# Running the second half of an expert slot one pair later in a layer with gathered experts

## What is computed

```python
mixed = gates[0] * (o_sb @ w_o_sb) + gates[1] * (o_sw @ w_o_sw) + gates[2] * (o_mem @ w_o_mem)
x = x + mixed @ w_out                       # the merge
q = (rmsnorm(x) @ w_q).reshape(t, 8, 2, 128)
s = einsum('thpd,hpkd->thpk', q, keys)      # 8 heads, 2 x 128 key scores
v1, i1 = top_k(s[:, :, 0], 16); v2, i2 = top_k(s[:, :, 1], 16)
best, flat = top_k(v1[..., :, None] + v2[..., None, :], 16)
idx = e1 * 128 + e2                         # 128 experts for each token
g = softmax(best)
a = gelu(einsum('thkd,td->thk', u_tab[idx], xb))
y = x + einsum('thk,thkd->td', g * a, v_tab[idx])
```

## Time and profile before

| | |
|---|---|
| median of 3 runs | 4426.72 us (4423.26 to 4434.2) |
| the profiled execution | 4421.1 us, its span 4419.2 us |
| busy: PE, DVE, ACT, POOL | 3611.0, 2811.9, 1235.3, 1836.7 us |
| granted TensorE clock, mean | 0.923 |
| moved by DMA | 1415.44 MB, of which 1208.03 MB by the gathers |
| 1152 gathers | first issued at 1145.6 us, last at 4389.4 us |
| DVE: 1152 dots of 1217 ns | idle before them 556.1 us, of which 548.7 us for a gather |
| PE: 3520 matmuls of L1375 | idle before them 688.4 us, of which 667.1 us for a diagonal |

### The profile page before, as it was taken

How to read it: one execution, slowest core, us unless ns; L and a number is a source line. 1 busy time by engine, 2 the same in 40 slices (tenths; PEclk the granted TensorE clock), 3 DMA queues, 4 the chain that set the end, 5 groups by cost and what they waited for, 6 DMA issues and landing times.

```text
span 4419.2 us, 34952 instructions
## 1 busy us (share of the span) xinstructions
PE 3611.0 (82%) x11113; PEld 1885.0 (43%) x11113; DVE 2811.9 (64%) x6038; ACT 1235.3 (28%) x2663; POOL 1836.7 (42%) x1477
## 2 busy tenths in 40 slices
PE   7999798989768797867898878996787777787777
PEld 4545457778534345432333335442233233233222
DVE  2130541821698965886996997687677676676554
ACT  2111772620332233332223224333111112112111
POOL 0000340000366576656666666666433333333332
PEclk9999996989889999988999999998899999999999
DMA  3202102234799899989999999999999999999998
GB/s 123 69 25 80 30 1 86 84 122 162 293 351 391 319 405 421 396 333 421 421 419 421 412 420 415 422 411 409 421 421 421 417 412 418 415 413 414 421 421 354
DMA packets 249160, 1415.44 MB, mean 320 GB/s; under 512 B 26624, under 2 KB 59648, under 8 KB 95872
## 3 DMA queue, kind: packets, MB, share of 16 engines
q0 software_dynamic: 165888, 1208.03, 66.6%
q1 hardware_dynamic: 83088, 205.18, 12.6%
HBM read 1374.85 MB, written 39.19 MB: 320 GB/s over the span
## 4 chain that ended last, share of the span: by engine, by line
DMA 23%; POOL 18%; DVE 13%; PE 12%; issue 11%; ACT 2%; POOLq 0%; SPq 0%; ACTq 0%; DVEq 0%
DMA ring<-in_experts_dram,idx 22%; POOL side L1265 10%; POOL ring L1254 8%; PE ps L1375 7%; DVE ring L1618 5%; PE ps L1298 2%; PE ps L1323 1%; DVE wgt L1624 1%; PE ps L1346 1%; PE ps L1308 1%; ACT diag L1468 1%; DVE hot L1507 1%; DVE hot L1510 1%; DVE e L1512 1%; DVE flat L1503 0%
## 5 line engine op out<-in xcount | busy, mean ns | idle before, releaser
L1375 PE MATMUL ps<-ring,diag 128*128 128x512 f32 x3520 | 1792.9, 654 | 688.4 <-ACT diag L1468 667.1
L1254 POOL DMA_INDIRECT ring<-in_experts_dram,idx x1152 | 1096.1, 952 | 1905.9 <-PE ps L1375 1334.5
L1618 DVE CUSTOM_DVE_ANT_0 ring<-ring,ps 128x1024 f32<-128x1024 f32 x1152 | 1381.7, 1217 | 556.1 <-DMA ring<-in_experts_dram,idx 548.7
L1375 PEld LDWEIGHTS ps<-ring,diag 128*128 128x128 f32 x3520 | 695.3, 206 | 1693.2 <-ACT diag L1468 948.7
L1265 POOL TENSOR_TENSOR side<-side,ring 128x1024 f32<-128x1024 f32 x272 | 640.8, 2356 | 42.6 <-ACT ring L1473 37.4
L1457 ACT ACTIVATE act_<-hid 128x2 f32<-128x2 f32 x576 | 117.1, 203 | 1773.5 <-DVE hid L1618 1772.8
L1468 ACT ACTIVATE diag<-const,wgt 128x128 f32<-128x128 f32 x880 | 319.4, 395 | 482.8 <-DVE wgt L1624 480.2
L1298 PE MATMUL ps<-hx,wbuf 128*128 128x256 f32 (+2 forms) x1152 | 403.1, 495 | 13.3 <-DMA hx<-hT_scratch 13.1
L1624 DVE TENSOR_TENSOR wgt<-act_,gw 128x2 f32<-128x2 f32 x576 | 240.9, 418 | 124.9 <-ACT act_ L1457 121.6
L1473 ACT ACTIVATE ring<-ring,wgt 128x1024 f32<-128x1024 f32 x272 | 308.4, 1134 | 0.0
L1298 PEld LDWEIGHTS ps<-hx,wbuf 128*128 128x128 f32 x1152 | 225.6, 196 | 184.5 <-issue 119.3
(11 more groups left out here) (187 smaller groups left out, 3096.6 us busy)
## 6 DMA issues: line engine op xcount, KB each, us to landing
wbuf<-in_w_gate_o_dram SPq DMA_DIRECT2D x72, 768.0 KB, 8.3
wbuf<-in_w_q_dram SPq DMA_DIRECT2D x24, 1024.0 KB, 9.0
ring<-in_experts_dram,idx POOLq DMA_INDIRECT x1152, 16.0
wbuf<-in_w_out_dram SPq DMA_DIRECT2D x12, 1024.0 KB, 8.9
w_qkv<-in_w_in_dram SPq DMA_DIRECT2D x5, 2048.0 KB, 8.0
o_x<-o_scratch SPq DMA_DIRECT2D x9, 768.0 KB, 25.2
s<-s_scratch SPq DMA_DIRECT2D x6, 1024.0 KB, 11.6
hT_scratch<-hT SPq DMA_DIRECT2D x9, 512.0 KB, 7.0
```

The lines of the kernel that those rows point to most:

```text
L1254: i = nc.gpsimd.indirect_dma_start(out=ring[:, j % RING, :], out_offset=None, in_=A["experts"], in_offset=bass.IndirectOffsetOnAxis(ap=idx ...
L1375: last = nc.tensor.matmul(acc[:, h, :], diag[:, (by_pe(j) - 1) % 4, :], ring[:, j % RING, DM + h * HB:DM + (h + 1) * HB], start=(j % SLOTS ...
L1618: last = nc.vector.tensor_tensor_reduce(out=u, in0=u, in1=xp, scale=1.0, scalar=0.0, op0=ALU.mult, op1=ALU.add, accum_out=hid[:, j % SLOTS ...
```

## The change

The pair of a slot's second half is now the pair before the one whose dots are being made. With Q = 64 m + q counting the pairs of all tiles:

- DVE: dots of Q, product of Q - 1, piece of the search, `finish` of the tile before (now at q = 1), advance. The last product stands alone behind the loop. The copy to `xp` waits for its own engine's `dots` as well.
- ACT: gelu of Q, then diagonals and scaled rows of Q - 1, then advance.
- PE: advance for Q, then the matmuls of Q - 1.

POOL and SP are as they were, and no instruction is added or taken away.

```diff
--- before.py
+++ after.py
@@ -1377,13 +1377,11 @@
                     last.then_inc(pe_done, 1)
 
             advance(0)
-            for m in range(NT):
-                for q in range(NB):
-                    if q == 0:
-                        advance(1 + m * NB)
-                    accumulate(m, q)
-                    if q:
-                        advance(1 + m * NB + q)
+            for Q in range(NT * NB + 1):
+                if Q < NT * NB:
+                    advance(1 + Q)
+                if Q:
+                    accumulate((Q - 1) // NB, (Q - 1) % NB)
 
         @block.scalar
         def _(act):
@@ -1450,27 +1448,33 @@
 
             advance = walk(front)
             advance(0)
-            for m in range(NT):
-                for q in range(NB):
+            def spread(m, q):
+                act.wait_ge(weights, m * NB + q + 1)
+                for j in range(m * SLOTS + q * BATCH, m * SLOTS + (q + 1) * BATCH):
+                    if sided(j):
+                        continue
+                    d = by_pe(j) - 1
+                    if d >= 4:
+                        act.wait_ge(pe_done, d - 3)
+                    last = nc.scalar.activation(diag[:, d % 4, :], ident, ACT.Copy, scale=wgt[:, j % SLOTS:j % SLOTS + 1])
+                last.then_inc(diags, 1)
+                for j in range(m * SLOTS + q * BATCH, m * SLOTS + (q + 1) * BATCH):
+                    if sided(j):
+                        v = ring[:, j % RING, DM:2 * DM]
+                        nc.scalar.activation(v, v, ACT.Copy, scale=wgt[:, j % SLOTS:j % SLOTS + 1]).then_inc(scaled, 1)
+
+            for Q in range(NT * NB + 1):
+                m, q = Q // NB, Q % NB
+                if Q < NT * NB:
                     c = slice(q * BATCH, (q + 1) * BATCH)
-                    act.wait_ge(dots, m * NB + q + 1)
+                    act.wait_ge(dots, Q + 1)
                     nc.scalar.activation(act_[:, c], hid[:, c], ACT.Gelu_apprx_tanh).then_inc(gelus, 1)
-                    advance(1 + m * NB + q)
+                if Q:
+                    spread((Q - 1) // NB, (Q - 1) % NB)
+                if Q < NT * NB:
+                    advance(1 + Q)
                     if q == TOP_FROM[m] + 24 * TOP_EVERY[m] + 1 and m + 1 < NT and m + 1 not in FIRST_OF:
                         exponentiate(m + 1, None)
-                    act.wait_ge(weights, m * NB + q + 1)
-                    for j in range(m * SLOTS + q * BATCH, m * SLOTS + (q + 1) * BATCH):
-                        if sided(j):
-                            continue
-                        d = by_pe(j) - 1
-                        if d >= 4:
-                            act.wait_ge(pe_done, d - 3)
-                        last = nc.scalar.activation(diag[:, d % 4, :], ident, ACT.Copy, scale=wgt[:, j % SLOTS:j % SLOTS + 1])
-                    last.then_inc(diags, 1)
-                    for j in range(m * SLOTS + q * BATCH, m * SLOTS + (q + 1) * BATCH):
-                        if sided(j):
-                            v = ring[:, j % RING, DM:2 * DM]
-                            nc.scalar.activation(v, v, ACT.Copy, scale=wgt[:, j % SLOTS:j % SLOTS + 1]).then_inc(scaled, 1)
 
         @block.vector
         def _(dve):
@@ -1594,6 +1598,12 @@
                         weigh(f.base, f.weigh[tau])
                     yield
 
+            def product(Q):
+                m, q = Q // NB, Q % NB
+                dve.wait_ge(gelus, Q + 1)
+                c = slice(q * BATCH, (q + 1) * BATCH)
+                nc.vector.tensor_tensor(wgt[:, c], act_[:, c], gw[:, m % 2, c], ALU.mult).then_inc(weights, 1)
+
             def finish(m):
                 last = m * SLOTS + SLOTS - 1
                 dve.wait_ge(pe_done, by_pe(last))
@@ -1607,6 +1617,8 @@
             spilled = 0
             for m in range(NT):
                 dve.wait_ge(x_in, 16 * (m + 1))
+                if m:
+                    dve.wait_ge(dots, m * NB)
                 nc.vector.tensor_copy(xp, xrow[:, :]).then_inc(x_taken, 1)
                 dve.wait_ge(x_taken, m + 1)
                 follow = m + 1 < NT and m + 1 not in FIRST_OF
@@ -1618,10 +1630,8 @@
                         last = nc.vector.tensor_tensor_reduce(out=u, in0=u, in1=xp, scale=1.0, scalar=0.0, op0=ALU.mult, op1=ALU.add,
                                                               accum_out=hid[:, j % SLOTS:j % SLOTS + 1])
                     last.then_inc(dots, 1)
-                    advance(1 + m * NB + q)
-                    dve.wait_ge(gelus, m * NB + q + 1)
-                    c = slice(q * BATCH, (q + 1) * BATCH)
-                    nc.vector.tensor_tensor(wgt[:, c], act_[:, c], gw[:, m % 2, c], ALU.mult).then_inc(weights, 1)
+                    if m or q:
+                        product(m * NB + q - 1)
                     c = q - TOP_FROM[m]
                     k = TOP_EVERY[m]
                     if follow and 0 <= c < 24 * k and c % k == 0:
@@ -1632,8 +1642,10 @@
                         shift(m + 1, None)
                     if follow and c == 24 * k + 2:
                         weigh(m + 1, None)
-                    if q == 0 and m:
+                    if q == 1 and m:
                         finish(m - 1)
+                    advance(1 + m * NB + q)
+            product(NT * NB - 1)
             finish(ST)
```

## The result

The change makes the kernel slower: 4472.85 us in the median of 4 runs (4469.81 to 4476.75) against 4425.0 of the kernel before beside it (4423.26 to 4434.2), a ratio of 1.0104 [1.0087, 1.0122]. The profiled execution took 4476.75 us, its span 4474.9, at a mean clock of 0.918. Forecast were 4435 us and a range from 4403 to 4468.

A forecast was written before the change was run, and what follows sets the result against it. Gathers were taken to bound the kernel behind 2030 us, VectorE three earlier stretches. Terms 0 + 0 + 5 + 15 + 3.7 - 4.5 - 5 - 6 = +8 us, against the 4426.7 median, gave 4435 us, range 4403 to 4468.

The forecast's parts named there:

- Tiles 2 to 4: ... I take 5 us: In tiles 2 to 4, gathers left with too little backlog lose 5 us, bounds 0 and 53 us.
- A slot's release moves by the same 4.7 us: Everywhere, a pair's product starts 4.7 us later, so its slot's release and next gather also come 4.7 us later.
- the 2.2 us for each piece: Tiles 2 to 4: most lost at each of 24 long search pieces, from the least gather latency; at most 53 us.
- Tiles 5 to 7, tile 8: 0: Tiles 5 to 8: gather latencies fall by 4.7 us but stay over 5.4, so the later release costs nothing.
- The tail: +3.7: Kernel end: the matmuls of the pair before run first, the last pair's follow, plus 3.7 us.
- Gelu waits: -4.5: Second and third stretches bound by VectorE: the product's wait for the gelu goes, 4.5 us saved.
- DVE's waits for ACT's merge steps: -5: Second and third stretches bound by VectorE: 12.2 us of waits shrink, 5 us saved, bounds -12 and some +5.
- The product held up by POOL's additions: -6: Stretches bound by VectorE: additions meet dots oftener and hold the product up less, 6 us saved, bounds -30 and +10.
- The three stretches: +15: 1196 to 1280, 1400 to 1560, 1840 to 1960 us, bound by VectorE: two fewer landed slots cost 5 us each time.
- The ring starves: Tiles 2 to 4 and the three stretches: ring of 10 too short, 4457 us at half the bound; chance 0.38.
- VectorE's relief wins: Three stretches bound by VectorE: fewer waits and hold-ups there win 28 us, 4399 us; chance 0.22.
- Nothing but the tail: Whole kernel: ring stays full, only 3.7 us added at the end, 4430 us; part of the case given 0.40.

The follow-up runs named there:

- lag_only: The changed kernel with the merge's steps put back where they were before, leaving only the lag of one pair: 4484.65 us, 1.0142 to the kernel before.
- after_ring11: The changed kernel with 11 ring slots instead of 10, three small search buffers moved into unused constants: 4439.72 us, 1.0039 to the kernel before.

## Why the prediction was wrong

**The failed step** is the term "Tiles 2 to 4: ... I take 5 us". It measured +44 (24.7 + 15.4 + 3.7). Two things in it were wrong.

The first is the row it leaned to. "Being nearer to the median's row" takes the median latency of the earlier trace rows, 4.5 us in hand; but a short queue comes back behind nearly every one of the 8 long pieces of a tile, and is paid there: 24.7/8 = 3.1 us for each in tile 2, 1.9 in tile 3, not the loss of a rare gather. A dip that comes with a period has to be priced at the least, whatever the median says.

The second is the step under it, "A slot's release moves by the same 4.7 us", for every pair. It holds for the median pair (product 0.28 us behind its dots before, 4.9 after), but not for the one ahead of a long piece: its product moved by 11.5 us in tile 2 and 8.9 in tile 3. So the 2.2 us for each piece were no upper bound. Tile 2 lost more than that; the 53 us hold 8 pieces of tile 4, which lost but 3.7, and the 16 of tiles 2 and 3 have a bound of 35 and lost 40.

With 44 in place of 5 the sum would have been +47; measured were 4472.85 - 4425.0 = +48. That they agree so well is in part luck, for the tiles add up to 55.7: the terms for the three stretches (15 - 4.5 - 5 - 6) forecast nothing, and tiles 0 and 1 lost 9.2.

Two things stood in the text and were passed over. At the long piece of tile 5 it says "the same gap now falls on the pair before, with one pair fewer under way". With the lag, the pair ahead of the piece is held across it, and PE has only the pair before that one to work on. What that does to a release was bounded there for tiles 5 to 7 and not carried over to tiles 2 to 4, where less is in hand. That PE stands still for 7 us and starts again at 1.2 GHz, with 8 matmuls in 6.62 us for 3.70, was not considered at all. And the item's other ground, "part of the delay there was paid already (ACT waited with its diagonals behind merge steps...)", holds only for tile 4: its long pieces, those of the next group's first search, stood between dots and product before the change too, and it lost 3.7 us.

**By its other steps:**

- *Tiles 5 to 7, tile 8: 0.* Right: -0.4, 0.0, -0.2 (tile 8's +3.3 is the tail), and 417 GB/s. There the pieces have the same instructions, but POOL adds almost nothing, the product ahead of a piece waits 8.4 us at most, and the backlog is deeper. The 4.7 us less latency show at the end: the last gather was issued at 4389.42 before and its dots started at 4408.80, 19.4 us later; after, 4447.56 to 4461.35 is 13.8. That is 5.6 less.
- *The tail: +3.7.* Right, +3.3. The last rows of the changed kernel, which answer to the earlier trace rows:

```profile
4461.35 1.22 DVE L1630 CUSTOM_DVE_ANT_0 ring<-ring,ps 128x1024 f32<-128x1024 f32 x1 [1.25 <-DMA ring<-in_experts_dram,idx]
...
4463.46 7.13 PE L1375 MATMUL ps<-ring,diag 128*128 128x512 f32 x16 [1.26 <-ACT diag L1459]
...
4470.63 1.23 DVE L1613 TENSOR_TENSOR side<-ps,side 128x1024 f32<-128x1024 f32 x1 [7.61 <-PE ps L1375]
```

  Sixteen matmuls for eight, and `finish` waits 7.61 us, where "some 8" was forecast.
- *Gelu waits: -4.5.* They are gone: the whole kernel has 0.2 us of them.
- *DVE's waits for ACT's merge steps: -5.* 2.5 us in the second stretch for 4.1, 2.3 in the third for 8.1, so -7.4: right. The waits of VectorE in the two stretches after:

```profile
DVE gt L1565 <- ACT gt L1401: 2.5, 2, 2.0
...
DVE v L1493 <- ACT mixn L1436: 2.3, 1, 2.3
```

- *The product held up by POOL's additions: -6.* Wrong in sign. The groups of 1150 to 1600, as in the earlier trace rows:

```profile
L1630 DVE CUSTOM_DVE_ANT_0 ring<-ring,ps 128x1024 f32<-128x1024 f32 x127 | 150.8, 1217 | 41.0 <-DMA ring<-in_experts_dram,idx 39.0 <-DVE gw L1544 1.2 <-DVE gw L1537 0.2
L1605 DVE TENSOR_TENSOR wgt<-act_,gw 128x2 f32<-128x2 f32 x62 | 54.6, 880 | 0.0
L1568 DVE TENSOR_TENSOR mixn<-mixn,gt 128x384 f32<-128x384 f32 x12 | 15.4, 1285 | 0.4
```

  880 ns for 753. The gate product fell from 1402 to 1285, but the product of a pair, moved right behind dots, is met oftener. The Trainium skill, "SBUF — State Buffer", "SBUF: two separate sides", has the mutual exclusion of a two-input operation of VectorE and an operation of GpSimd that reads SBUF, and the product's mean (172 ns without additions) agrees. The sum of it could not be had from the rule: who meets whom is set by the order, and I had guessed it. The cast of 2.86 us in the timeline above, 0.18 us in the timeline of before, ends as the addition beside it does (2477.54 and 2477.48); it has one input, so the two-input case isn't what held it, and no run here shows which condition did.
- *The three stretches: +15.* Tiles 0 and 1 hold them and lost 9.2 us together, with the held-up product among it. That ring length counts there is shown: an eleventh slot wins 13.8 us in those tiles, 8 slots cost 22.6, and lag_only, without the merge's new place, loses 17.6. The price was of the right order; no run has it apart from what else changed there.

**The rivals.** "The ring starves" was right, in its place (tiles 2 to 4) and in what meets there (long pieces, scaled rows); its 4457 us took half of the bound of 53 where 44 came. It had 0.38, and the range ended "somewhat past half of its bound" for no better reason than that. "VectorE's relief wins" failed because nothing of VectorE's held-up time was relieved: its busy time rose from 2811.9 to 2827.3 us. "Nothing but the tail" doesn't hold even with a ring of 11 and the piece cut: against the kernel before with the same edits some 15 us are left, most of them in tiles 0 and 1.

**What stays open:** whether the lower clock has any part in the 40 us of tiles 2 and 3 (14 at most by one pair of profiles, which the totals don't confirm), and how much of a dip is the additions' hold on the piece. Counted from the traces, the 8 pieces of tile 2 take 62.6 us together before and 72.8 in the changed kernel, with 0 and 5 casts held up, so up to 10 of that tile's 24.7 us may be this. In tile 3 they take 70.2 and 66.4 us, so there the hold isn't the cause of the loss.

## What to carry to other kernels

Before a stage is run one unit behind another, look for the longest thing on the engine between two units: the unit ahead of it is held across it, so the ring must cover the piece plus the lag. It is the least backlog behind each such piece that is to be compared, times their number, not the median, and with the delay of the unit ahead of the piece (12 us here), not that of the usual one (4.7). If the ring can't grow, cut the piece or catch up ahead of it; each alone took the 40 us down to 4. A wait that a lag removes is worth nothing while the transfers set the pace, and a step that hides a wait shouldn't be moved away from it (the merge's steps hid 50 us of gelu). And when two edits make up for a change, give them to the kernel before as well: only that comparison shows what the change still costs.

## What the runs showed of the hardware

- The granted clock falls in a stretch that is bound by transfers, with and without the change: 0.81 and 0.85 in the two windows of the kernel before, 0.52 and 0.54 in those of the changed kernel and of lag_only. Behind 6.7 us without a matmul PE came back at the lower level, and 8 matmuls took 6.62 us for 3.70. That this costs time isn't shown: after_ring11 has as much of the lower clock in tiles 2 and 3 as the changed kernel and half of its loss.
- The gathers' rate falls before the DMA share does: 377 us at a share of 0.98 moved 394 GB/s, where 1.01 moved 420.
- A cast of 128x32 from uint32 to float32 on VectorE, one input, took 2.86 us beside an addition of POOL and 0.18 without. Dots with one input in PSUM stayed at 1217 ns.
- A float32 matmul of 512 columns is two rows of 0.43 us at the upper clock: 12 of them were 10.3 us for a place.
